# Spreading the first norm weights with whole-array products, and splitting the first two weight parts before the first copy

## The chip, the cores and the metric

One NeuronCore of one Trainium2 chip runs the whole program. The metric is the device time of one execution in microseconds (us); lower is better. Engines are named as in the profile: PE is TensorE (PEld its weight loads), DVE is VectorE, ACT is ScalarE, POOL is GpSimd, and SP is SyncE, which here only issues transfers.

## The reference, cut to what matters

Three transformer layers on one sequence of 256 tokens with 1024 features, all in fp32: attention and a squared-ReLU MLP, then two layers with modulation. The change touches the first lines of the first layer only:

```python
def rms_norm(x, gain):
    xf = x.astype(jnp.float32)
    y = xf * lax.rsqrt(jnp.mean(xf * xf, axis=-1, keepdims=True) + RMS_EPS)
    return (y * gain.astype(jnp.float32)).astype(x.dtype)

u = rms_norm(h, norm_mix_pre[layer])       # h = x, 256 x 1024
q, k, v = jnp.split(u @ w_qkv, 3, axis=-1) # w_qkv 1024 x 3072
```

## The kernel before

Every engine has its own written program, and semaphores order them. The tokens are two tiles (t = 0, 1) of 128 rows. Weights come in parts of 128 partitions by 1024 floats, 512 KB each, that SP loads in a fixed order into the slots of `w_raw`. ACT copies a part, rounded to fp32r, into `w_hi` (`split_part` of ACT, L721 to L727), and DVE subtracts that from the raw part and writes the rest to `w_lo` (`split_part` of DVE, L1160 to L1163). PE then multiplies high by high, high by rest and rest by high part. Activations are split in the same way: PE transposes the normed tile `xn` into PSUM (`norm_T`, L1917), ACT copies four blocks of it as the high part of `aT` (`norm_hi`, L776), and DVE takes the rest (`norm_lo`, L1170). A slot is loaded anew only when DVE has taken its rest.

The order of the work at the start, before the loops, is written out by hand on each engine:

- SP issues tile 0 of x, weight parts 0 and 1, tile 1 of x, parts 2 and 3, and then parts 4 and on as slots come free.
- POOL fills `eps` and `ones` (128x128 of 1.0), and then other constants, and counts `consts`.
- ACT issues the transfer of the 1024 norm weights (L811): half of them to partition 0 and half to partition 64 of `gain`. It loads its function table (L816), sums the squares of tile 0 (L737), takes ln (L822) and exp (L823) for `rstd`, splits part 0, copies the first four transposed blocks, splits part 1, and goes on to tile 1.
- PE runs three products of `ones` by `ones` (`warm_up(3)`, L2142). When the norm weights are there it spreads each half over all 128 partitions with a product that has one row: stationary `ones[q, :]`, moving `gain[q, 0, 0:CH]`, with q partition 0 for the first and partition 64 for the second (L2148). After one more product of ones it begins `first_entry`: transposes of tile 0, the products of parts 0 and 1 with it, transposes of tile 1, and the rest (L2022).
- DVE waits for the product of each half and for `rstd`, and writes `xn` = x * rstd * spread weights, read from PSUM (L1430), two instructions a tile. Between the tiles come the rests of part 0, of the first blocks of `aT`, and of part 1.

The lines around it on PE:

```python
warm_up(3)
pe.wait_ge(gain_loaded[0], 16)
for n in range(2):
    q = slice(n * P // 2, n * P // 2 + 1)
    pe.matmul(acc[:, 2 + n, :], ones[q, :], gain[q, 0, 0:CH], start=True, stop=True).then_inc(gain_spread, 1)
warm_up(1)
pe.wait_ge(consts, 2)
first_entry(U_QKV1, (acc[:, 0, :], acc[:, 1, :]))
```

Of the kernel before, what the change touches and what calls it, by code (L numbers as in the profile page):

```python
# [32 lines left out]
P = 128  # L33
# [4 lines left out]
CH = 512  # L38
# [72 lines left out]
def plus(base, i, per):  # L111

    return base if i is None else i * per + base


def block_program(nc, a, out):
    ctx = ExitStack()
    with ctx:
        def sb(name, shape, dt=F32):
            return ctx.enter_context(nc.sbuf_tensor(name, shape, dt))  # L120

        def ps(name, shape):
            return ctx.enter_context(nc.psum_tensor(name, shape, F32))

        def sem(name):
            return ctx.enter_context(nc.semaphore(name))
# [14 lines left out]
        gain = sb("gain", [P, 4, D])  # L141
# [3 lines left out]
        ones = sb("ones", [P, P])  # L145
# [66 lines left out]
        acc = ps("acc", [P, 4, CH])  # L212
# [55 lines left out]
        def rounded_part(v):  # L268

            return apart[v][0] if v in apart else w_hi[:, slot_of(v), :]  # L270
# [20 lines left out]
        def norm_banks(k, t):  # L291

            if k in NORMS_T:
                return [acc[:, 2 * t, :], acc[:, 2 * t + 1, :]]
            if k == 1:
                return [acc[:, 0, :], acc[:, 1, :]]
            if k == 2:
                return [tp[:, 0, :], tp[:, 1, :]]
            return [ub[:, 0, :], ub[:, 1, :]] if t else [tp[:, 0, :], tp[:, 1, :]]
# [2 lines left out]
        x_loaded = [sem("x_loaded0"), sem("x_loaded1")]  # L302
        rows_loaded = sem("rows_loaded")
        small_loaded = sem("small_loaded")
        gain_spread = sem("gain_spread")
        gain_loaded = [sem(f"gain_loaded{n}") for n in range(8)]
        w_loaded = [sem(f"w_loaded{n}") for n in range(SLOTS)]
# [101 lines left out]
        def blocks(w):  # L409
# [7 lines left out]
        gains = [a["norm_mix_pre"][0], a["norm_mix_post"][0], a["norm_ffn_pre"][0], a["norm_ffn_post"][0],  # L417
                 a["l0_mix_norm_2"], a["l0_ffn_norm_2"], a["l1_mix_norm_2"], a["l1_ffn_norm_2"]]
# [288 lines left out]
        def _(act):  # L707
            n_chain = [0]

            def chained(ins):  # L710
                n_chain[0] += 1
                ins.then_inc(act_chain, 1)
                act.wait_ge(act_chain, n_chain[0])
# [7 lines left out]
            def split_part(v, i=None, per=0):  # L721
                act.wait_ge(w_loaded[v % SLOTS], plus(16 * (v // SLOTS + 1), i, 16 * 2 * per // SLOTS))
                if v in before_in_slot:
                    act.wait_ge(w_used, before_in_slot[v] + 1)
                elif v >= SLOTS:
                    act.wait_ge(w_used, plus(v - SLOTS + 1, i, 2 * per))
                act.activation(rounded_part(v), w_raw[:, v % SLOTS, :], ACT.Copy).then_inc(hi_done, 1)  # L727
# [7 lines left out]
            def row_square(t, src):  # L735
                n_sq[0] += 1
                act.activation(squares[:, t, :], src, ACT.Square, accum_out=sums[:, t:t + 1]).then_inc(sq_done, 1)  # L737
# [34 lines left out]
            def norm_hi(k, t, groups=(0, 1)):  # L772

                for g in groups:
                    act.wait_ge(nT_done, 4 * k + 2 * t + g + 1)
                    act.activation(aT_hi[:, 4 * g:4 * g + 4, t * P:(t + 1) * P],  # L776
                                   norm_banks(k, t)[g].rearrange("p (b n) -> p b n", n=P), ACT.Copy).then_inc(n_hi, 1)
# [30 lines left out]
                act.wait_ge(w_used, parts_to(u + 2))  # L808
                act.activation(vtok[:, 0, n * CH:(n + 1) * CH], acc[:, 2 * n, :], ACT.Copy).then_inc(v_a, 1)

            act.dma_start(gain[0:P:P // 2, 0, 0:CH], gains[0].rearrange("(a n) -> a n", a=2)).then_inc(gain_loaded[0], 16)  # L811

            def first_norm(u):

                n_norm[0] += 1
                act.preload_act_table_set("natural_log_exp_and_others")  # L816
                act.wait_ge(consts, 1)
                for t in range(NT):
                    act.wait_ge(x_loaded[t], 16)
                    row_square(t, x[:, t, :])  # L820
                    act.wait_ge(sq_done, n_sq[0])
                    chained(act.activation(log_var[:, t:t + 1], sums[:, t:t + 1], ACT.Ln, scale=1.0 / D, bias=eps[:, 0:1]))  # L822
                    act.activation(rstd[:, t:t + 1], log_var[:, t:t + 1], ACT.Exp, scale=-0.5).then_inc(rstd_done, 1)  # L823
                    if t == 0:
                        split_part(2 * u)
                        norm_hi(0, 0, (0,))
                        split_part(2 * u + 1)
                norm_hi(0, 0, (1,))
                split_part(2 * u + 2)
                norm_hi(0, 1)  # L830
                split_part(2 * u + 3)

            first_norm(U_QKV1)
            act.activation(ones_r[:, :], ones[:, :], ACT.Copy)

# [310 lines left out]
        def _(dve):  # L1146
# [13 lines left out]
            def split_part(v, i=None, per=0):  # L1160
                dve.wait_ge(hi_done, hi_count(v, i, per))
                dve.tensor_tensor(rest_part(v), w_raw[:, v % SLOTS, :], rounded_part(v).bitcast(F32),  # L1162
                                  ALU.subtract).then_inc(lo_done, 1)  # L1163
# [26 lines left out]
            def norm_lo(t, q):  # L1190

                k = n_norm[0]
                n_norm[0] += t * q
                dve.wait_ge(n_hi, 4 * k + 2 * t + q + 1)
                part = (slice(None), slice(4 * q, 4 * q + 4), slice(t * P, (t + 1) * P))
                bank_lo(aT_lo[part], aT_hi[part], norm_banks(k, t)[q].rearrange("p (b n) -> p b n", n=P)).then_inc(n_lo, 1)
# [224 lines left out]
            def copy_v(u, n):  # L1421
                dve.wait_ge(w_used, parts_to(u + 2))
                dve.tensor_copy(vtok[:, 1, n * CH:(n + 1) * CH], acc[:, 2 * n + 1, :]).then_inc(v_v, 1)

            for t in range(NT):
                n_rstd[0] += 1
                dve.wait_ge(rstd_done, n_rstd[0])
                for c in range(2):
                    dve.wait_ge(gain_spread, c + 1)
                    dve.scalar_tensor_tensor(xn[:, t, c * CH:(c + 1) * CH], x[:, t, c * CH:(c + 1) * CH], rstd[:, t:t + 1],  # L1430
                                             acc[:, 2 + c, :], ALU.mult, ALU.mult).then_inc(xn_done, 1)
                if t == 0:
                    split_part(2 * U_QKV1)
                    norm_lo(0, 0)
                    split_part(2 * U_QKV1 + 1)
# [363 lines left out]
        def _(pe):  # L1799
# [339 lines left out]
            def warm_up(n):  # L2139

                for _ in range(n):
                    pe.matmul(ub[:, 0, :], ones[:, :], ones[:, :].unsqueeze(1).broadcast_to([P, 4, P]), start=True, stop=True)  # L2142

            warm_up(3)
            pe.wait_ge(gain_loaded[0], 16)
            for n in range(2):
                q = slice(n * P // 2, n * P // 2 + 1)
                pe.matmul(acc[:, 2 + n, :], ones[q, :], gain[q, 0, 0:CH], start=True, stop=True).then_inc(gain_spread, 1)  # L2148
            warm_up(1)
            pe.wait_ge(consts, 2)  # L2150
            first_entry(U_QKV1, (acc[:, 0, :], acc[:, 1, :]))

# [247 lines left out]
            for step, n in STICK_STEPS:  # L2400
# [27 lines left out]
                elif step == "W":  # L2428
# [3 lines left out]
                    for e in range(2):  # L2432
                        for b in range(3):
                            q = slice(e * SC + b * P, e * SC + (b + 1) * P)
# [37 lines left out]
```

## Time and profile before

| | us |
|---|---|
| median of 3 runs | 890.13 |
| lowest and highest | 889.53, 890.37 |
| the profiled execution's own time | 890.48 |
| its span in the profile | 888.4 |
| PE busy | 882.0 (99%) |
| DVE busy | 694.2 (78%) |
| ACT busy | 501.6 (56%) |
| POOL busy | 29.0 (3%) |

The span is that of one profiled execution; the rest of its own time, 2.1 us, lies around the span. Start times count from the start of the span. A row of the timeline merges neighbouring instructions of one kind: with x6 the length is that from the first's start to the last's end. A plain fp32 product appears as two records with the moving operand's 512 columns each.

### The profile page before, as it was taken

The numbers are of one execution on the slowest core, as the hardware profiler recorded it, in microseconds if no ns is written. First come the engines' busy times: TensorE is split into PE (matmuls) and PEld (weight loads), VectorE is DVE, ScalarE is ACT, GpSimd is POOL, SyncE is SP. The second block draws the span as 40 slices with busy tenths as digits, with TensorE's granted clock in tenths as the row PEclk, the third lists the DMA queues.
The fourth block names the chain that finished last, engine by engine and source line by source line (L and its number), as shares of the span: only waits on it lengthen the run. The fifth ranks groups of instructions, "written<-read, shape, count | busy, mean of one in ns | idle before, by whom it ended". The sixth has DMA issues, their size and how long they took to land.

```text
span 888.4 us, 13272 instructions
## 1 busy us (share of the span) xinstructions
PE 882.0 (99%) x4841; PEld 747.3 (84%) x4841; DVE 694.2 (78%) x735; ACT 501.6 (56%) x673; POOL 29.0 (3%) x52
## 2 busy tenths in 40 slices
PE   9999999999999999999999999999999999999998
PEld 5998878888888799979888888878777888888886
DVE  5698977988888987896888888687797875655655
ACT  6545665565555758756455455465775565545542
POOL 4000110000000100001000000010000000000000
PEclk9999999999999999999999999999999999999999
DMA  7979586899998385556988888636434366666661
GB/s 239 343 254 346 171 297 196 320 366 355 340 332 335 122 285 152 186 185 191 364 311 318 321 311 283 192 115 208 133 117 142 118 212 193 190 189 189 189 191 69
DMA packets 117093, 208.04 MB, mean 234 GB/s; under 512 B 7237, under 2 KB 81069, under 8 KB 111930
## 3 DMA queue, kind: packets, MB, share of 16 engines
q1 hardware_dynamic: 116566, 205.31, 67.9%
q10 hardware_dynamic: 292, 2.10, 0.7%
q8 instruction: 28, 0.46, 0.2%
q14 instruction: 15, 0.12, 0.0%
q0 software_dynamic: 192, 0.05, 0.0%
HBM read 206.39 MB, written 1.05 MB: 233 GB/s over the span
## 4 chain that ended last, share of the span: by engine, by line
PE 94%; DVE 3%; DMA 1%; issue 1%; ACT 0%; SPq 0%; DVEq 0%; POOL 0%; ACTq 0%; POOLq 0%
PE ub L1945 11%; PE tp L1945 10%; PE acc L1845 7%; PE acc L1846 7%; PE acc L1848 7%; PE ub L1947 5%; PE acc L1808 5%; PE tp L1947 5%; PE acc L1810 5%; PE acc L1809 5%; PE tp L1965 4%; PE acc L1931 3%; PE acc L1933 3%; PE acc L1932 3%; PE acc L1965 2%; PE acc L2022 1%
## 5 line engine op out<-in xcount | busy, mean ns | idle before, releaser
L1162 DVE TENSOR_TENSOR w_lo<-w_raw,w_hi 128x1024 fp32r<-128x1024 f32 x283 | 341.7, 1222 | 104.5 <-ACT w_hi L727 104.0
L727 ACT ACTIVATE w_hi<-w_raw 128x1024 fp32r<-128x1024 f32 x283 | 296.8, 1057 | 214.0 <-PE acc L1848 49.6
L1945 PE MATMUL tp<-aT,w_hi 128*128 128x512 f32 x432 | 135.9, 396 | 0.0
L1945 PE MATMUL ub<-aT,w_hi 128*128 128x512 f32 x432 | 135.4, 395 | 0.0
L1845 PE MATMUL acc<-w_hi,hT_hi 128*128 128x512 f32 x284 | 110.8, 390 | 0.7 <-DVE w_lo L1162 0.7
L1846 PE MATMUL acc<-w_lo,hT_hi 128*128 128x512 f32 x284 | 110.6, 389 | 0.0
L1848 PE MATMUL acc<-w_hi,hT_lo 128*128 128x512 f32 x272 | 105.8, 389 | 0.0
L1947 PEld LDWEIGHTS tp<-aT,w_lo 128*128 128x128 f32 x432 | 81.2, 188 | 19.2
L1947 PEld LDWEIGHTS ub<-aT,w_lo 128*128 128x128 f32 x432 | 81.1, 188 | 18.9
L1947 PE MATMUL tp<-aT,w_lo 128*128 128x256 f32 x432 | 84.9, 278 | 0.0
L1947 PE MATMUL ub<-aT,w_lo 128*128 128x256 f32 x432 | 84.9, 278 | 0.0
L1945 PEld LDWEIGHTS ub<-aT,w_hi 128*128 128x128 f32 x432 | 67.6, 189 | 2.0
L1945 PEld LDWEIGHTS tp<-aT,w_hi 128*128 128x128 f32 x432 | 65.8, 189 | 0.0
L1808 PE MATMUL acc<-w_hi,aT 128*128 128x512 f32 x160 | 64.4, 402 | 0.0
L1845 PEld LDWEIGHTS acc<-w_hi,hT_hi 128*128 128x128 f32 x284 | 53.3, 188 | 11.2 <-DVE w_lo L1162 0.7
L1810 PE MATMUL acc<-w_hi,aT 128*128 128x512 f32 x160 | 62.4, 390 | 0.0
L1809 PE MATMUL acc<-w_lo,aT 128*128 128x512 f32 x160 | 62.4, 390 | 0.0
L1846 PEld LDWEIGHTS acc<-w_lo,hT_hi 128*128 128x128 f32 x284 | 53.3, 188 | 10.1
L1848 PEld LDWEIGHTS acc<-w_hi,hT_lo 128*128 128x128 f32 x272 | 51.1, 188 | 10.8
L1372 DVE SCALAR_TENSOR_TENSOR mod<-ada_raw,silu_c,mod 128x2048 f32<-128x2048 f32 x24 | 56.3, 2346 | 0.2 <-DVE mod L1372 0.2
L1931 PE MATMUL acc<-aT,w_hi 128*128 128x256 f32 x192 | 55.3, 288 | 0.0
L1933 PE MATMUL acc<-aT,w_lo 128*128 128x256 f32 x192 | 54.3, 283 | 0.0
(330 smaller groups left out, 1309.8 us busy)
## 6 DMA issues: line engine op xcount, KB each, us to landing
ada_raw<-in_l_ada_w SPq DMA_DIRECT2D x24, 1024.0 KB, 6.5
w_raw<-in_l_ffn_w_gate SPq DMA_DIRECT2D x44, 512.0 KB, 4.6
w_raw<-in_l_ffn_w_up SPq DMA_DIRECT2D x44, 512.0 KB, 3.9
w_raw<-in_l_ffn_w_down SPq DMA_DIRECT2D x44, 512.0 KB, 3.6
w_raw<-in_w_up SPq DMA_DIRECT2D x32, 512.0 KB, 5.2
w_raw<-in_w_down SPq DMA_DIRECT2D x32, 512.0 KB, 5.6
scratch<-in_l_ada_w SPq DMA_DIRECT2D x14, 1024.0 KB, 7.8
w_raw<-in_attn_w_qkv SPq DMA_DIRECT2D x24, 512.0 KB, 6.8
```

The source lines that it names most:

```text
L727: act.activation(rounded_part(v), w_raw[:, v % SLOTS, :], ACT.Copy).then_inc(hi_done, 1)
L1162: dve.tensor_tensor(rest_part(v), w_raw[:, v % SLOTS, :], rounded_part(v).bitcast(F32), ALU.subtract).then_inc(lo_done, 1)
L1808: pe.matmul(outp, op_hi[:, k + n, q], wh[:, c], start=start and n == 0, stop=False)
L1809: pe.matmul(outp, op_hi[:, k + n, q], wl[:, c], start=False, stop=False)
L1810: last = pe.matmul(outp, op_lo[:, k + n, q], wh[:, c], start=False, stop=stop and n == 1)
L1845: pe.matmul(outp, operand[0][:, k, q], wh[:, c], start=start, stop=False)
L1846: last = pe.matmul(outp, operand[0][:, k, q], wl[:, c], start=False, stop=False)
L1848: last = pe.matmul(outp, operand[1][:, k, q], wh[:, c], start=False, stop=stop)
L1931: pe.matmul(outp, wh, aT_hi[:, b, :], start=b == 0, stop=False)
L1933: last = pe.matmul(outp, wl, aT_hi[:, b, :], start=False, stop=b == KB - 1)
L1945: pe.matmul(banks[f], rounded_part(v)[:, c[f]], aT[:, :, b, :], start=b == 0, stop=False)
L1947: last = pe.matmul(banks[f][:, 0:TOK], rest_part(v)[:, c[f]], aT_hi[:, b, :], start=False, stop=b == KB - 1)
```

## The change

Four edits, all at the start of the program:

1. DVE clears the whole of `gain[:, 0, :]` (128x1024 fp32) and counts a new semaphore, `gain_cleared`.
2. ACT waits for it, and then issues the transfer of all 1024 norm weights to partition 0, in place of two halves to two partitions.
3. PE runs two products of ones in place of three, spreads each half with a product that takes all 128 partitions (127 of them zeros), and runs no product of ones behind them.
4. ACT splits weight part 1 ahead of the first copy of transposed blocks, where it came behind it.

```diff
@@ -808,7 +809,8 @@
-            act.dma_start(gain[0:P:P // 2, 0, 0:CH], gains[0].rearrange("(a n) -> a n", a=2)).then_inc(gain_loaded[0], 16)
+            act.wait_ge(gain_cleared, 1)
+            act.dma_start(gain[0:1, 0, :], gains[0].rearrange("(a n) -> a n", a=1)).then_inc(gain_loaded[0], 16)
@@ -823,8 +825,8 @@
                     if t == 0:
                         split_part(2 * u)
+                        split_part(2 * u + 1)
                         norm_hi(0, 0, (0,))
-                        split_part(2 * u + 1)
@@ -1422,6 +1424,7 @@
+            dve.memset(gain[:, 0, :], 0.0).then_inc(gain_cleared, 1)
             for t in range(NT):
@@ -2141,12 +2144,11 @@
-            warm_up(3)
+            warm_up(2)
             pe.wait_ge(gain_loaded[0], 16)
             for n in range(2):
-                q = slice(n * P // 2, n * P // 2 + 1)
-                pe.matmul(acc[:, 2 + n, :], ones[q, :], gain[q, 0, 0:CH], start=True, stop=True).then_inc(gain_spread, 1)
-            warm_up(1)
+                pe.matmul(acc[:, 2 + n, :], ones[:, :], gain[:, 0, n * CH:(n + 1) * CH], start=True,
+                          stop=True).then_inc(gain_spread, 1)
             pe.wait_ge(consts, 2)
```

The order on ACT from its first transfer on, before (`nT_done` counts the groups of four transposed blocks, `w_loaded0` and `w_loaded1` the landings of weight parts 0 and 1):

```order
L811 DMA gain<-in_norm_mix_pre 2x512
L816 ACT_TABLE_LOAD
L737 ACTIVATE scratch,sums<-x 128x1024 [waits x_loaded0,consts]
L822 ACTIVATE log_var<-sums,eps 128x1 [waits sq_done]
L823 ACTIVATE rstd<-log_var 128x1 [waits act_chain]
L727 ACTIVATE w_hi<-w_raw 128x1024 [waits w_loaded0]
L776 ACTIVATE aT<-tp 128x4x128 [waits nT_done]
L727 ACTIVATE w_hi<-w_raw 128x1024 [waits w_loaded1]
L737 ACTIVATE scratch,sums<-x 128x1024 [waits x_loaded1]
```

and of the change:

```order
L813 DMA gain<-in_norm_mix_pre 1x1024 [waits gain_cleared]
L818 ACT_TABLE_LOAD
L738 ACTIVATE scratch,sums<-x 128x1024 [waits x_loaded0,consts]
L824 ACTIVATE log_var<-sums,eps 128x1 [waits sq_done]
L825 ACTIVATE rstd<-log_var 128x1 [waits act_chain]
L728 ACTIVATE w_hi<-w_raw 128x1024 [waits w_loaded0]
L728 ACTIVATE w_hi<-w_raw 128x1024 [waits w_loaded1]
L777 ACTIVATE aT<-tp 128x4x128 [waits nT_done]
L738 ACTIVATE scratch,sums<-x 128x1024 [waits x_loaded1]
```

The transfer has a wait ahead of it, and the second split stands ahead of the copy of the transposed blocks.

The order on PE from its first product on, before (`ub` and `acc` are banks of PSUM):

```order
L2142 MATMUL ub<-ones 128x512 [waits consts]
L2142 MATMUL ub<-ones 128x512 x2
L2148 MATMUL acc<-gain,ones 128x512 [waits gain_loaded0]
L2148 MATMUL acc<-gain,ones 128x512
L2142 MATMUL ub<-ones 128x512
L1917 MATMUL tp<-ident,xn 128x128 [waits xn_done,consts]
```

and of the change:

```order
L2145 MATMUL ub<-ones 128x512 [waits consts]
L2145 MATMUL ub<-ones 128x512
L2150 MATMUL acc<-gain,ones 128x512 [waits gain_loaded0]
L2150 MATMUL acc<-gain,ones 128x512
L1920 MATMUL tp<-ident,xn 128x128 [waits xn_done,consts]
```

One product of ones is gone ahead of the wait for the norm weights and one behind the two spreading products.

## Rows read from the trace of the kernel before

**Rows 1.** The page's first part: busy us, share of the span, instructions.
```profile
PE 882.0 (99%) x4841; PEld 747.3 (84%) x4841; DVE 694.2 (78%) x735; ACT 501.6 (56%) x673; POOL 29.0 (3%) x52
```

**Rows 2.** Waits of PE from 17 us to the end: us in total, times, longest.
```profile
PE acc L1845 <- DVE w_lo L1162: 0.7, 2, 0.5
PE acc L2166 <- issue: 0.3, 1, 0.3
```

**Rows 3.** The chain of waits, start to 130 us: start us, us, what.
```profile
1.02 5.31 PE ub L2142 x6
6.32 1.06 PE acc L2148 x4
7.38 1.06 PE ub L2142 x2
8.44 0.60 PE tp L1917 x4
...
10.61 0.14 issue
10.74 2.54 PE acc L2022 x10
13.28 1.07 PE ub L1917 x8
...
117.05 0.86 PE ub L2250 x2
```

**Rows 4.** Timeline of PE's weight loads and matmuls: start us, us, instruction.
```profile
3.74 0.34 PEld L2142 LDWEIGHTS ub<-ones 128*128 128x128 f32 x1 [0.52 <-issue]
4.59 0.34 PEld L2142 LDWEIGHTS ub<-ones 128*128 128x128 f32 x1 [0.52 <-issue]
...
5.44 0.88 PE L2142 MATMUL ub<-ones 128*128 128x512 f32 x1
```

**Rows 5.** Timeline of DVE, 0 to 15 us.
```profile
7.50 1.41 DVE L1430 SCALAR_TENSOR_TENSOR xn<-x,rstd,acc 128x512 f32<-128x512 f32 x2 [7.50 <-PE acc L2148]
8.82 1.22 DVE L1162 TENSOR_TENSOR w_lo<-w_raw,w_hi 128x1024 fp32r<-128x1024 f32 x1
10.63 1.23 DVE L1162 TENSOR_TENSOR w_lo<-w_raw,w_hi 128x1024 fp32r<-128x1024 f32 x1
12.24 1.41 DVE L1430 SCALAR_TENSOR_TENSOR xn<-x,rstd,acc 128x512 f32<-128x512 f32 x2 [0.38 <-ACT rstd L823]
```

**Rows 6.** Timeline of ACT, 0 to 12.5 us, and one row of 27 us.
```profile
0.74 1.11 ACTq L811 DMA_DIRECT2D gain<-in_norm_mix_pre  x1
1.88 1.28 ACT L816 ACT_TABLE_LOAD   x1 [1.88 <-issue]
5.90 0.20 ACT L823 ACTIVATE rstd<-log_var 128x1 f32<-128x1 f32 x1
6.00 1.04 ACT L727 ACTIVATE w_hi<-w_raw 128x1024 fp32r<-128x1024 f32 x1
9.06 0.60 ACT L776 ACTIVATE aT<-tp 128x512 fp32r<-128x512 f32 x1 [2.01 <-PE tp L1917]
9.55 1.05 ACT L727 ACTIVATE w_hi<-w_raw 128x1024 fp32r<-128x1024 f32 x1
10.50 1.05 ACT L737 ACTIVATE scratch<-x 128x1024 f32<-128x1024 f32 x1
12.00 0.20 ACT L823 ACTIVATE rstd<-log_var 128x1 f32<-128x1 f32 x1
...
27.10 1.06 ACT L727 ACTIVATE w_hi<-w_raw 128x1024 fp32r<-128x1024 f32 x1 [2.86 <-DMA w_raw<-in_attn_w_qkv]
```

**Rows 7.** DMA issues in 0 to 1.5, 2 to 2.5 and 6.5 to 7 us: us to landing.
```profile
x<-in_x SPq DMA_DIRECT2D x1, 512.0 KB, 3.6
...
x<-in_x SPq DMA_DIRECT2D x1, 512.0 KB, 6.5
...
mod<-in_l_ada_b POOLq DMA_DIRECT2D x1, 8.0 KB, 4.5
```

**Rows 8.** The queue of ACT's transfer, the last stretch with a packet of it (3.8 to 3.9 us).
```profile
q10 hardware_dynamic: 1, 0.00, 0.6%
```

**Rows 9.** Groups by shape: fills and copies near to the added one: xcount | busy us, mean ns.
```profile
L1408 DVE COPY scratch<-acc 128x512 f32<-128x512 f32 x2 | 1.4, 688 | 1.5 <-PE acc L2022 1.5
L666 POOL MEMSET rg_w<- 128x1024 f32 x1 | 1.0, 952 | 0.1
```

**Rows 10.** One stretch: us, busy of each engine, PEclk, DMA share, GB/s.
```profile
1.00:4.00 3.00, 2.98 (x4) 1.44 (x5) 0.00 (x0) 1.28 (x1) 2.36 (x8) 1.00 0.68 231
```

More of the change, by code:

```diff
@@ L304, in block_program @@
         small_loaded = sem("small_loaded")
+        gain_cleared = sem("gain_cleared")
         gain_spread = sem("gain_spread")
```

## The prediction

> **What bounds the kernel now.** I read the page's busy shares first: PE is busy 882.0 of 888.4 us, and no other engine comes near [rows 1]. Then the waits of PE alone: from 17 us to the end it waits 1.0 us in three places [rows 2]. So behind the start the time is PE's own work, and whatever time PE gains or loses at the start stays in the total. Then the chain of waits at the start [rows 3]: three products of ones from 1.02 to 6.32, the two spreading products to 7.38, one product of ones to 8.44, transposes, then a broken stretch until 13.28, where the transposes of tile 1 begin. From there the chain stays on PE. The place to predict is therefore the start of tile 1's transposes, 13.28 (modelled end of the work before; the engine's own start is at about 13.1).
>
> What sets that start? DVE. Its first instruction begins at 7.50, 0.12 us after the spreading products end; it then runs two `xn` instructions, three rests and again two `xn` with a single gap of 0.38 us, for tile 1's `rstd` [rows 5]. PE has idle moments before 13.1 and takes tile 1's `xn` when it comes. ACT had `rstd` of tile 0 ready at 6.10 [rows 6], 1.4 us before DVE could use it, because PE was still multiplying ones: that is the slack this change can reach. And tile 1's `rstd` is late because ACT sums its squares only from 10.50, behind a split that itself waited behind the copy of blocks at 9.06 [rows 6], though tile 1 of x had landed at about 2.18 + 6.5 = 8.7 [rows 7].
>
> **The clear and the transfer.** DVE does nothing before 7.50, so the clear itself costs DVE nothing; but the transfer waits for it, and ACT's table load waits behind the transfer. A DVE clear of 128x1024 does not occur in the trace. Near it stand a POOL clear of that size, 0.95 us, a DVE copy of half the size, 0.69 us, and a DVE subtraction of the full size, 1.22 us [rows 5, 9]; I bound it by 0.5 and 1.25 and take 1.05, nearest to the POOL clear. The Trainium skill, page "VectorE: DVE Perf Modes", section "Zero memsets can be issued as uint32 (trn2)", says that a memset takes one cycle per element whatever the type, which rules out that a clear runs at several elements a cycle; no run here shows it yet. If the engines begin at 0.74 as ACT does [rows 6], the clear ends at about 1.8 and the transfer is issued from 1.8 to 2.9, if it takes its 1.11 us again. The table load then runs from about 2.95 to 4.25, and tile 0 of x lands at 0.74 + 3.6 = 4.34 [rows 7]. So on ACT the 1.05 us are hidden, with only 0.1 us left; anything more (a clear of 1.25) pushes `rstd` from 6.10 by as much, and that is not yet the latest input of DVE (below). POOL's `ones` do not touch the same buffer; I cost their clash with the clear at nothing.
>
> When does the row land? Before, the last packet of ACT's queue came by 3.9 us [rows 8], 3.15 after the issue began; landing is not recorded, as nobody waited. From 1.8 on, the same delay gives 4.95, and with about 0.15 for the notice I take 5.1. Lower bound: tile 0 of x took 3.6 us for 128 times the data, so the small one may take under 3: 4.5. Upper: the 8 KB transfer that POOL issued at 6.8 under the same load took 4.5 us [rows 7]: 6.3.
>
> **PE.** The passes of a ones product start 0.855 us apart (3.74 to 4.59) [rows 4], while later fp32 products of the same size take 0.86 us for two, 0.43 each [rows 3]: a factor of two, so PE starts at the 1.2 GHz level although the granted clock of that stretch reads 1.00 [rows 10]. The last pass from 5.44 is only 0.88 long [rows 4] where 1.06 is usual, and from 6.32 records follow each other every 0.53. So I place the rise at about 6.15, after 5.1 us of unbroken products. With two products of ones, PE is done at 1.02 + 4 x 0.855 = 4.44. It then idles until 5.1, 0.66 us that it did not idle before. The spreading products before ran side by side: 1.06 us for both [rows 3]. Over the whole array they run one after the other: 1.06 each at the pace behind the rise (bounds 0.86, the later products, and 1.71, at the low level). The first: 5.1 to 6.15 at the low level is 61% of it, the rest 0.41, end 6.56; the second ends at 7.62. The removed product of ones behind them cost 1.06 on PE, but no one waited for it: the transposes waited for `xn` all the same.
>
> **DVE.** `xn` of the first half starts at 6.7, the second at 7.62 + 0.12 = 7.74 and ends at 8.48; before, the pair ended at 8.91. That is 0.43 earlier. The three rests take 8.91 to 11.86 before, 2.95 us, so now end at 11.43. The gap of 0.38 should go: ACT has part 0 split at 7.05 and part 1, by the reordering, at 8.1; the first blocks are transposed at about 8.25 and copied at 8.87, so the copy does not suffer from the split ahead of it, and x of tile 1 has landed, so its squares start at 8.87 in place of 10.50 and its `rstd` is ready at 10.6, well before 11.43. So `xn` of tile 1 starts at 11.43 in place of 12.24: 0.81 us earlier.
>
> **PE again.** Before tile 1's transposes PE has ten products of 0.225 us: they can start at about 9.1 with nothing to wait for between parts 0 and 1 (the 0.14 at 10.61 [rows 3] goes), then wait for the rest of part 1 until 11.43, and end at 11.9; tile 1's first half comes at 12.2. So PE is ready, and the transposes start 0.8 us earlier. What comes late next? ACT's copies and parts 2 and 3 move with the chain. Loads of part 4 and later wait for slots that DVE frees, so they move as well, and where ACT waits for a load, as for 2.86 us before 27.10 [rows 6], PE needs the part only some 5 us later, after the products of parts 6 and 7. I take nothing off there.
>
> The sum against the profiled execution is 890.48 - 0.8 = 889.7. That execution was 0.35 us above the median; against the median of 890.13 it is 889.35, which I forecast as 889.4. A measurement of this kernel can tell about 0.2% from no change, 1.8 us; so this gain would be within it.
>
> **A rule against it.** The rise of PE's clock is the weak point: of the 6.15 - 1.02 us in which PE worked without a pause before, it would now rest 0.66. The trace shows one rise, and not where it comes with a pause. The Trainium skill, page "TensorE: Matmul & The Clock Gate", section "What's actually happening", says that activity releases the throttle and that the measuring window runs free of the kernel's start. By that rule the rise comes at another point in each execution, and a pause can move it to a later one; the sentences that follow price this from rows.
>
> **The rivals.**
> *1. The clock rises late.* PE stays at the low level past the pause. The spreading products then take 3.42 us and end at 8.5, `xn` of the second half starts at 8.64, its end is 0.47 later than before and with the 0.38 gap gone tile 1's `xn` starts 0.1 later than before. If the clock rises there (9 to 10 us), that is all: +0.1 to +0.3. If it stays low beyond, the ten products take 4.3 us in place of 2.25, and PE reaches tile 1's transposes at about 14 in place of 13.1, transposes and products after that losing 0.5 us for each further us at the low level: +1.4 by 14 us, and over +1.8 only if it lasts to about 15. For it: the pause, and the shorter run of ones. Against: the pause is short, and full-array products run on both sides of it, 3.4 us of them ahead. Time: 890.3, or 891.5 in the longer form.
> *2. The row lands late.* At 6.3 in place of 5.1, with the clock up at 6.15, the products end at 8.4 and everything before is undone: 890.1. With the clock low, it is the longer form of rival 1. The row decides from 6.3 on.
> *3. The row lands early*, by 4.5. The products end at about 7.3, 0.3 earlier, and `xn` follows; or they run at 0.86 each, another 0.2 to 0.3. Time 888.9.
> *4. The lead is taken back* by a load or by PE's later waits, which are for rests of weights [rows 2]: 890.1. Against it are the spare us before each early part.
>
> **How the numbers follow.** The forecast (a lead of 0.5 to 0.9) has 0.45, rival 3 0.15, rival 1's short form 0.13 and its longer form 0.10, rival 2 0.07, rival 4 0.10. The range leaves out the far end of the longer form and a lead over 1.6: 888.5 to 891.0. Faster by over 1.8 us would need more than all of DVE's early wait for PE (1.4 us from 6.10) and the 0.38 gap together, 0.04; slower by that much needs the clock low to 15 us, 0.05; the rest, 0.91, is within.
>
> **What would show it.** DVE's clear of about 1.05 us from 0.74; ACT's transfer from 1.8; PE idle from 4.44 to about 5.1; spreading products ending near 6.6 and 7.6; `xn` of tile 1 at 11.4 with no gap ahead of it for `rstd`; two splits in a row on ACT from 6.0; tile 1's transposes at 12.3. Wrong would be: passes 0.855 apart behind 6.5 us, a pause of PE over 1.5 us, or a wait of `xn` of tile 1 for ACT.

## The result, and the profile after

The change made the kernel slower: 892.64 us (median of 18 runs, 890.0 to 894.45) against 890.29 us (18 runs, 889.53 to 891.07), a ratio of 1.0025 with a 95% interval of 1.0018 to 1.0031. I had forecast 889.4, with a range up to 891.0. Not only the middle moved: the runs of after spread over 4.45 us, three times as wide as those of before.

The profiled execution took 892.91 us, 2.43 more than that of before. The page shows the same work in a longer span: PE is busy 0.7 us more, and idle for 1.7 us more.

```profile
span 890.8 us, 13265 instructions
PE 882.7 (99%) x4837; PEld 748.3 (84%) x4837; DVE 694.8 (78%) x736; ACT 501.9 (56%) x673; POOL 29.0 (3%) x52
```

PE's waits from 17 us to the end add up to 1.2 us, as against the 1.0 of [rows 2]. So most of the loss arises before 17 us, and the chain of waits (start us, us, what) shows it; it answers to [rows 3].

```profile
1.02 0.92 DVE gain L1427
1.94 0.02 issue
1.97 4.71 DMA gain<-in_norm_mix_pre
6.68 0.04 issue
6.72 3.78 PE acc L2150 x4
10.51 1.96 PE tp L1920 x8
12.46 2.95 PE acc L2025 x12
15.41 0.87 PE ub L1920 x8
```

The clear, 0.92 us, then the transfer of 4 KB, 4.71 us, then the two spreading products, 3.78 us (1.06 for both before), then eight transposes in 1.96 (four took 0.60). Tile 1's transposes end the list: they start at 15.41, where they started at 13.28, 2.1 us later. The timeline of after (start us, us, instruction, and the idle time ahead of it) gives the engines beside it, as [rows 5, 6] did:

```profile
1.97 0.53 ACTq L813 DMA_DIRECT2D gain<-in_norm_mix_pre  x1
2.54 1.28 ACT L818 ACT_TABLE_LOAD   x1 [2.54 <-DVE gain L1427]
5.64 0.20 ACT L825 ACTIVATE rstd<-log_var 128x1 f32<-128x1 f32 x1
6.72 3.78 PE L2150 MATMUL acc<-gain,ones 128*128 128x512 f32 x4 [1.92 <-DMA gain<-in_norm_mix_pre]
8.14 1.06 ACT L728 ACTIVATE w_hi<-w_raw 128x1024 fp32r<-128x1024 f32 x1 [1.36 <-DMA w_raw<-in_attn_w_qkv]
10.54 0.75 DVE L1433 SCALAR_TENSOR_TENSOR xn<-x,rstd,acc 128x512 f32<-128x512 f32 x1 [0.87 <-PE acc L2150]
14.07 1.40 DVE L1433 SCALAR_TENSOR_TENSOR xn<-x,rstd,acc 128x512 f32<-128x512 f32 x2
15.25 1.04 PE L1920 MATMUL ub<-ident,xn 128*128 128x128 f32 x8
```

PE stands idle for 1.92 us until the row (the 1024 norm weights, all on partition 0) lands. `rstd` of tile 0 is ready at 5.84; the second half of tile 0's `xn` begins at 10.54. The gap ahead of tile 1's `xn` is indeed gone (no idle time at 14.07, 0.38 before), but the whole chain is 1.8 us late. The spreading products run at the 1.2 GHz level: their passes start 0.85 apart (7.74 and 8.59 in the next rows), as those of the ones did. The trace's own list of clock levels begins only when the clock rises: at 12.74 us here, at 6.02 in the trace of before.

```profile
7.74 0.34 PEld L2150 LDWEIGHTS acc<-gain,ones 128*128 128x128 f32 x1 [0.52 <-issue]
8.59 0.34 PEld L2150 LDWEIGHTS acc<-gain,ones 128*128 128x128 f32 x1 [0.52 <-issue]
```

### The profile page after: what moved, and what is told of

The parts are those of the page before. It is cut to its first block, busy times and chain, and to the rows that moved or that the text cites. A ratio compares the mean times of both kernels' runs of the same rounds, so it can differ in the third digit from the quotient of the medians.

```text
span 890.8 us, 13265 instructions
## 1 busy us (share of the span) xinstructions
PE 882.7 (99%) x4837; PEld 748.3 (84%) x4837; DVE 694.8 (78%) x736; ACT 501.9 (56%) x673; POOL 29.0 (3%) x52
## 3 DMA queue, kind: packets, MB, share of 16 engines
HBM read 206.39 MB, written 1.05 MB: 233 GB/s over the span
## 4 chain that ended last, share of the span: by engine, by line
PE 93%; DVE 4%; DMA 1%; issue 1%; ACT 1%; SPq 0%; DVEq 0%; ACTq 0%
PE ub L1948 11%; PE tp L1948 10%; PE acc L1848 7%; PE acc L1849 7%; PE acc L1851 7%; PE ub L1950 5%; PE acc L1811 5%; PE tp L1950 5%; PE acc L1812 5%; PE acc L1813 5%; PE tp L1968 3%; PE acc L1934 3%; PE acc L1936 3%; PE acc L1935 3%; PE acc L1968 2%; PE acc L2025 1%
```

## The experiments

Three theories were set against each other. **C**: the late row opens a pause of PE, the pause keeps the clock low, and the low clock is most of the loss. **R**: the late row costs it by itself. **S**: whole-array products in series cost it, at any clock. Each run below was timed beside the kernel before on the same chip; the medians of before in the three groups of several kernels were 890.26, 890.34 and 890.11. Each kernel ran eleven times. The ratios and intervals are those on record; they are not the ratio of the two medians, and differ from it by up to 0.0008.

**The third product of ones put back.** In the changed kernel:

```diff
-            warm_up(2)
+            warm_up(3)
             pe.wait_ge(gain_loaded[0], 16)
```

> The changed kernel with its third product of ones put back ahead of the wait for the norm weights. Theory C (the clock: PE's pause of about 2 us between the ones and the late row keeps it at the low level until about 10.5 us, and that is most of the loss): PE is busy to 6.32, the row lands at about 6.7, so the clock is up and the two spreading products take about 2.1 us and end near 8.8; xn of tile 1 begins near 12.5 and the time is 890.2 to 890.9. Theory R (the late row itself costs it, the clock little): about 892, as the changed kernel. Theory S (whole-array products one after the other are the cost, at any clock): 891.3 or more.

Measured: 890.82 us (890.0 to 891.3), ratio to before 1.0006 (0.9997 to 1.0015). The row landed as late as in after, at 6.71, but the clock was up:

```profile
6.76 1.98 PE L2150 MATMUL acc<-gain,ones 128*128 128x512 f32 x4 [0.86 <-DMA gain<-in_norm_mix_pre]
12.31 1.40 DVE L1433 SCALAR_TENSOR_TENSOR xn<-x,rstd,acc 128x512 f32<-128x512 f32 x2
13.12 1.30 PE L1920 MATMUL ub<-ident,xn 128*128 128x128 f32 x8
```

The same two products, after a wait that ended at the same time, take 1.98 us in place of 3.78, and tile 1's transposes start at 13.12, exactly as in the timeline of before (15.25 in that of after). One product of ones, work that no one uses, takes 1.8 us off the median of after (892.64 less 890.82; 1.7 by the two ratios to before). That is theory C, and it leaves about 0.5 us to R and S together, with whatever the new order of splits gives or takes.

**The wait alone.** In the kernel before (two halves, one-row products, three ones):

```diff
+            act.wait_ge(gain_cleared, 1)
             act.dma_start(gain[0:P:P // 2, 0, 0:CH], ...)
...
+            dve.memset(gain[:, 0, :], 0.0).then_inc(gain_cleared, 1)
```

> The kernel before with only the clear on DVE and the transfer's wait for it (two halves on two partitions, one-row products, three ones and one, the old order of splits). Theory C: the row lands near 6.7 in place of 4, but PE is covered by ones until 6.32, so the spreading products start 0.4 later: 890.5 to 890.8. Theory R: 892 or more. Theory S: 890.3, as before.

Measured: 891.6 us (891.17 to 892.28), ratio 1.0015 (1.0006 to 1.0024): between my figures for C and for R, 0.8 too slow for C as I had written it. The trace of this kernel shows a part of the reason, and it is the only trace here whose granted clock leaves 1.00 before PE's work is over. The view by stretches (stretch, us, busy and count of PE, PEld, DVE, ACT and POOL, granted clock, DMA share, GB/s):

```profile
9.00:12.60 3.60, 3.60 (x13) 2.71 (x13) 3.26 (x4) 2.41 (x4) 3.01 (x4) 0.53 0.71 249
12.60:16.00 3.40, 3.40 (x21) 2.77 (x20) 2.59 (x5) 2.93 (x8) 0.13 (x1) 1.00 0.80 259
```

The clock had risen, at 5.69 by the trace's list of levels, and it fell back to half from 9.10 to 12.52. What PE had done before it fell stands in the timeline: 0.78 us of pause, 1.1 us of one-row products, one product of ones.

```profile
6.95 1.13 PE L2151 MATMUL acc<-gain,ones 1*128 1x512 f32 x4 [0.78 <-DMA gain<-in_norm_mix_pre]
8.00 1.12 PE L2145 MATMUL ub<-ones 128*128 128x512 f32 x2
9.08 1.93 PE L1920 MATMUL tp<-ident,xn 128*128 128x128 f32 x8
```

So the clear and the wait cost 1.3 us over before even without the other edits. The fall is not in every run: the clock averaged over the whole run is 0.997 or 0.998 in four of the eleven (median 891.96) and 0.999 or 1.000 in the other seven (median 891.3). So about 1.0 us of the loss is there without a fall.

**That kernel with a fourth product of ones.**

```diff
-            warm_up(3)
+            warm_up(4)
```

> The kernel with only the clear and the wait (one-row products, two halves), with a fourth product of ones ahead of the row's wait. In the trace of that kernel the clock had risen by 6.0, PE paused from 6.2 to 6.9, the one-row products followed, and from 9.1 to about 12.6 PE ran at the low level again. If the pause with one-row products behind it took the clock down, covering it with ones keeps the clock up: tile 1's transposes begin near 13.8 in place of 14.5 and the time is 890.6 to 891.1, against 891.6. If the late row alone made that kernel slow, the time stays at 891.4 to 891.8.

Measured: 891.37 us (890.92 to 892.29), ratio 1.0017 (1.0008 to 1.0026). This does not tell the two figures apart. In its trace the clock stays up (eight transposes in 1.22 us where they took 1.93), but the four products of ones now last until 7.47 themselves, and the spread starts 0.45 us later than without the fourth, though the norm weights had landed at 6.65; tile 1's transposes begin at 14.29 against 14.54. In that execution the filler costs nearly what it saves. The average clock is 1.000 in all eleven runs, and still five of them lie at 891.86 or above. How much of the 1.3 us is clock stays open.

**The split order undone,** in the changed kernel: `norm_hi(0, 0, (0,))` between the two splits again.

> The changed kernel with the split of part 1 behind the first copy again. The order of splits was to take away the gap ahead of tile 1's xn, 0.38 us. Theories C, R and S all say: 0 to 0.8 us slower than the changed kernel, 892.6 to 893.4. If the split ahead of the copy is itself a cause of the loss, it is faster than the changed kernel by 0.3 or more.

Measured: 892.34 us (890.36 to 893.28), ratio 1.0021 (1.0012 to 1.0030): 0.3 below the median of after, well inside either spread. The order of the splits is not a cause of the loss that can be measured. Its profiled execution shows something else: the same transfer, issued at 1.96, landed after 3.56 us here and after 4.71 in after's. PE's pause was 0.77 us in place of 1.92, and the products were at the low level all the same; the clock rose at 9.45.

```profile
1.96 3.56 DMA gain<-in_norm_mix_pre
```

**The split order alone,** in the kernel before:

```diff
                         split_part(2 * u)
+                        split_part(2 * u + 1)
                         norm_hi(0, 0, (0,))
-                        split_part(2 * u + 1)
```

> The kernel before with only the order of ACT changed: the split of part 1 ahead of the first copy. The gap of 0.38 us ahead of tile 1's xn goes, if part 1 has landed by 7.05; nothing else moves: 889.8 to 890.1. If part 1 lands only at 8.1, as in the changed kernel's trace, the split ends at 9.2, the copy of the first blocks starts 0.1 later, and the rstd of tile 1 is still 0.7 earlier than before: the same 0.3 to 0.4 us.

Measured: 889.77 us (889.57 to 890.88) beside 890.34, ratio 1.0001 (0.9992 to 1.0010). It was run once more:

> The kernel before with only the split of part 1 ahead of the first copy, once more, beside the others of this batch. The first time it stood 0.57 us below the median of before: again 889.6 to 890.0 if that is real, 890.2 to 890.5 if it was not.

Measured: 890.21 us (889.24 to 891.08) beside 890.11, ratio again 1.0001 (0.9992 to 1.0010). The first lead was not repeated; the edit is worth nothing that can be told. The timeline of the first of the two shows where about half of the 0.38 us went:

```profile
8.19 1.06 ACT L727 ACTIVATE w_hi<-w_raw 128x1024 fp32r<-128x1024 f32 x1 [1.43 <-DMA w_raw<-in_attn_w_qkv]
9.79 1.20 PE L2022 MATMUL acc<-w_hi,aT 128*128 128x512 f32 x4 [0.70 <-ACT aT L776]
11.51 1.40 DVE L1430 SCALAR_TENSOR_TENSOR xn<-x,rstd,acc 128x512 f32<-128x512 f32 x2
```

Part 1 of the weights lands at 8.17, so the split waits 1.43 us for it, and the copy of the transposed blocks, ready since about 8.5, waits behind the split; PE then waits 0.70 us for the copy. The gap ahead of tile 1's `xn` is gone, and in its place stands a wait for a load: tile 1's `xn` begins 4.54 us behind tile 0's, where it was 4.74, so 0.2 us is left of it.

**The row ahead of the weights.** In the changed kernel SP issues the row between tile 0 of x and weight part 0:

```diff
             load_x(0)
+            sp.wait_ge(gain_cleared, 1)
+            sp.dma_start(gain[0:1, 0, :], ...).then_inc(gain_loaded[0], 16)
             proj_half(U_QKV1, qkv1, 0, 0)
...
-            act.wait_ge(gain_cleared, 1)
-            act.dma_start(gain[0:1, 0, :], ...).then_inc(gain_loaded[0], 16)
```

> The changed kernel with the row issued by SP right behind tile 0 of x and ahead of weight part 0, behind the same clear, which SP now waits for; weight parts 0 and on are issued about 0.8 us later. If the row is late because it stands behind the 1.5 MB of x and weights queued ahead of it, it lands by 4.6; then PE has no pause of more than 0.2 us, the clock rises near 6.15, the products end near 7.3 and the time is 889.5 to 890.3. If small transfers simply take about 4.7 us from their issue at this time, it lands at 6.7 and the time is 892 to 893.

Measured: 890.11 us (889.67 to 892.47), ratio 1.0002 (0.9993 to 1.0011); ten of eleven runs are at 891.05 or below. Same clear, same wait, same issue time (1.96), but nothing but tile 0 of x ahead in the transfers, and the row is there at 4.95:

```profile
1.96 0.31 SPq L505 DMA_DIRECT2D gain<-in_norm_mix_pre  x1
5.00 2.37 PE L2150 MATMUL acc<-gain,ones 128*128 128x512 f32 x4 [0.20 <-DMA gain<-in_norm_mix_pre]
```

It took 3.0 us from its issue, against 4.7. In this kernel SP held the weight parts back as well, so the run shows that the load ahead of a small transfer sets when it lands, and not how the engines share themselves out.

This kernel is nearly the case that I had forecast: the row at 4.95 (5.1 forecast), the clock up at 5.80 (6.15), tile 1's transposes at 12.40, 0.7 us earlier than before. The median is 0.15 below before, and not 0.8. The profiled execution, one of the two slowest, shows one way in which such a lead is lost: it took 891.05, 0.6 more than that of before. PE waits in it for a later norm:

```profile
PE acc L1920 <- DVE xn L1189: 1.0, 2, 0.7
378.77 5.80 DMA w_raw<-in_l_ffn_w_gate
```

The first line is of its waits from 17 us on, where before has no such wait; the second is of its chain of waits, and the `xn` of the longer of the two waits stands behind this load. Counted on DVE's instructions it is 0.8 ahead of before at 60 us, 0.6 ahead at 360 and 0.6 behind at 395. How often this happens, the other ten runs can't tell.

**Two products of ones and an early row.** In the kernel before, `warm_up(3)` becomes `warm_up(2)`, and nothing else:

> The kernel before with two products of ones ahead of the row in place of three, all else as before (one-row products side by side, one product of ones behind them). The row lands near 4.2, so there is no pause; the spreading products start at 4.5. If one-row products keep PE as busy to the clock as whole ones, the clock rises near 6.15, the spread is there at 6.2, xn starts at 6.3 and the time is 889.1 to 889.6. If they do not count, the clock rises later, and the time is 890.5 to 892 with a wide spread between executions.

Measured: 890.98 us (889.33 to 892.21), ratio 1.0007 (0.9998 to 1.0016). The runs fall in two groups: two at 889.33 and 889.78, the other nine from 890.92 up. There is no pause in its trace, the norm weights having landed at 4.01, before the ones end, and yet the clock is late:

```profile
4.73 2.08 PE L2148 MATMUL acc<-gain,ones 1*128 1x512 f32 x4
6.73 2.08 PE L2142 MATMUL ub<-ones 128*128 128x512 f32 x2
8.60 1.92 PE L1917 MATMUL tp<-ident,xn 128*128 128x128 f32 x8
10.35 2.23 PE L2022 MATMUL acc<-w_hi,aT 128*128 128x512 f32 x4
```

The clock rises at 12.59, and everything until then runs at half pace. PE was as busy as in before; what replaced whole-array ones from 4.8 to 6.8 was one-row products. They fill time but did not raise the clock here. The last kernel below has whole-array products in that place, and none of its 22 runs is above 890.4; it differs in other things too.

**One-row products between ones,** an attempt at beating both: two ones ahead, two behind, and the new split order.

> The kernel before with the one-row products side by side put between two products of ones ahead and two behind them, and the split of part 1 ahead of the first copy: an attempt at beating both. The row is there at 4.4; at the low level the two products take 1.7 us and end near 6.2, when rstd is ready too; xn starts at 6.3 in place of 7.5. PE is busy with ones to about 8.0. With the clock up near 6.2: 888.9 to 889.4. If the two ones behind delay the first transposes (xn's first half is there at 7.05): 889.4 to 889.9. If one-row products do not count for the clock: 890.5 or more.

Measured: 891.39 us (888.87 to 892.4), ratio 1.0005 (0.9996 to 1.0015). Again two groups: four runs from 888.87 to 889.75 and seven from 891.35 up. Its lowest run is the lowest of all on record. The profiled execution is one of the seven: the clock rises at 10.54, the ones behind the spread run from 6.81 to 10.52 at half pace, and the transposes wait behind them. That the four fast runs are those in which the clock rose early is likely, but no trace shows one of them.

**The row on one partition, no clear.** In the kernel before the whole row goes to partition 0, and both one-row products read it there:

> The kernel before with the whole row on partition 0 and both one-row products there, so they can't run side by side; no clear, no wait, three ones and one. The second product ends 1.06 us later than before if the pace behind the rise is kept, xn of the second half starts at 8.5 in place of 8.2: 0.2 to 0.4 us slower than before, 890.5 to 890.7 (theory S would have 891.3 or more from this alone).

Measured: 890.72 us (890.05 to 891.35), ratio 1.0008 (0.9999 to 1.0017). The products took 1.98 us one after the other where they had taken 1.06 side by side. It is 0.4 slower at the median, as expected, and not above what can be told: by the interval it is 1.5 us at most. So theory S is worth little, and the last kernel, which has whole-array products in series and is the fastest, says the same. This trace also shows how fast the row can be: 4 KB to one partition, issued at 0.74 with only tile 0 of x beside it, landed at 2.60.

**The idea without the wait.** In the changed kernel the transfer itself writes the norm weights to 32 partitions, at the start, and DVE clears the other 96; the stationary operand holds 1/32 (`spread` is 128 columns of scratch that POOL fills). PE waits for the clears and for POOL, and the transfer waits for nothing:

```diff
-            act.wait_ge(gain_cleared, 1)
-            act.dma_start(gain[0:1, 0, :], ...)
+            act.dma_start(gain[0:32, 0, :], gains[0].partition_broadcast(32)).then_inc(gain_loaded[0], 16)
...
-            dve.memset(gain[:, 0, :], 0.0).then_inc(gain_cleared, 1)
+            dve.memset(gain[32:64, 0, :], 0.0).then_inc(gain_cleared, 1)
+            dve.memset(gain[64:P, 0, :], 0.0).then_inc(gain_cleared, 1)
...
             warm_up(2)
+            pe.wait_ge(gain_cleared, 3)
             pe.wait_ge(gain_loaded[0], 16)
...
-                pe.matmul(acc[:, 2 + n, :], ones[:, :], gain[:, 0, n * CH:(n + 1) * CH], start=True,
+                pe.matmul(acc[:, 2 + n, :], spread[:, :], gain[:, 0, n * CH:(n + 1) * CH], start=True,
```

> The changed kernel without its wait: the row is broadcast by the transfer to partitions 0 to 31 (128 KB), issued by ACT at the start as before; DVE clears only partitions 32 to 127, in two instructions, and the stationary operand is 1/32 in place of 1 in the spreading products, which still take all 128 partitions. If the wait is what made the changed kernel slow, the rows land near 4.5 to 5, there is no pause over 0.5 us, the clock rises near 6, the products end near 7.3: 889.4 to 890.2. If whole-array products after only two products of ones are slow in themselves, 891 or more.

Measured: 889.34 us, eleven runs from 889.29 to 889.58, ratio 0.9992 (0.9983 to 1.0001). And again:

> The kernel that loads the norm weights to 32 partitions without a wait, once more, to see if its lead is real: 889.2 to 889.6 and all executions within 0.5 us of each other if xn of tile 0 waits for rstd and no longer for PE, so that the point at which the clock rises does not matter; 889.8 to 890.5 with a spread as wide as that of before if the first result was luck.

Measured: 889.56 us (889.18 to 890.37) beside 890.68, ratio 0.9990 (0.9981 to 0.9999). The spread is narrower than that of before, though the second time it was 1.2 us and not the 0.5 I had named. The timeline of the first:

```profile
0.75 0.41 ACTq L814 DMA_DIRECT2D gain<-in_norm_mix_pre  x1
4.59 2.00 PE L2153 MATMUL acc<-gain,scratch 128*128 128x512 f32 x4
5.09 1.06 ACT L740 ACTIVATE scratch<-x 128x1024 f32<-128x1024 f32 x1 [2.61 <-DMA x<-in_x]
6.83 1.41 DVE L1435 SCALAR_TENSOR_TENSOR xn<-x,rstd,acc 128x512 f32<-128x512 f32 x2 [3.73 <-ACT rstd L826]
11.03 1.40 DVE L1435 SCALAR_TENSOR_TENSOR xn<-x,rstd,acc 128x512 f32<-128x512 f32 x2
12.17 1.03 PE L1922 MATMUL ub<-ident,xn 128*128 128x128 f32 x8
```

The norm weights for 32 partitions, 128 KB, landed at 4.37. They are not free: tile 0 of x lands 0.7 us later than in before, at 5.0, and `rstd` with it. But the spread is ready at 6.6, before `rstd` at 6.79, so `xn` no longer waits for PE. That is, as I read it, why the point at which the clock rises matters less, and why the runs agree. By its median this is the fastest of the kernels that were run, 0.8 and 1.1 us ahead of before, about 0.1%: beyond noise in one of the two comparisons and at its edge in the other.

**The profiled executions side by side** (us; landings by the semaphore events, rises by the list of clock levels, starts by the timelines; one execution each, and the rise differs from one to the next):

| kernel | norm weights landed | spread begins | clock rises | tile 1's transposes | time |
|---|---|---|---|---|---|
| before | 4.17 | 6.25 | 6.02 | 13.12 | 890.48 |
| third product of ones back | 6.71 | 6.76 | 5.14 | 13.12 | 890.82 |
| wait alone | 6.90 | 6.95 | 5.69, falls 9.10, rises 12.52 | 14.54 | 892.15 |
| row ahead of the weights | 4.95 | 5.00 | 5.80 | 12.40 | 891.05 |
| 32 partitions, no wait | 4.37 | 4.59 | 4.78 | 12.17 | 889.29 |
| split order undone | 5.52 | 5.57 | 9.45 | 14.00 | 891.56 |
| after | 6.68 | 6.72 | 12.74 | 15.25 | 892.91 |
| two ones, one-row products | 4.01 | 4.73 | 12.59 | 14.34 | 891.43 |

## Why the prediction was wrong

The forecast was 0.8 us faster; after is 2.35 us slower at the median. Two steps failed: the landing of the row, and with it the rise of the clock. Two of the three signs that I had named for being wrong came: passes 0.85 apart behind 6.5 us, and a pause of PE over 1.5 us. Step by step:

- **What bounds it**: right in the main. The time is decided before tile 1's transposes. They came 2.1 us late, and the profiled executions differ by 2.4. But I had written that whatever PE gains or loses at the start stays in the total, and that holds only to some tenths: counted on DVE's instructions, after is 2.0 behind at 60 us and 2.4 from 395 us on, and the kernel with the row ahead of the weights lost its lead on the way.
- **The clear**: 1.05 us expected, 0.91 measured. DVE began at 1.02 and not at 0.74, so it ended at 1.93 in place of 1.8. The Trainium skill, page "VectorE: DVE Perf Modes", section "Zero memsets can be issued as uint32 (trn2)", has a clear take one cycle per element whatever the type. The traces agree in so far as no clear was faster than 0.91 us for 1024 elements a partition, over 32, 64 or 128 partitions alike; only fp32 was cleared, so what it says of the type no run here shows.
- **ACT behind it**: better than expected. With one partition to write, the issue took 0.53 us in place of 1.11, and `rstd` was ready at 5.84.
- **The landing of the row**: the first step that failed. I took 5.1 and an upper bound of 6.3; it landed at 6.68. I carried the delay of before, 3.15 us from issue to last packet [rows 6, 8] and 0.15 for the notice, over to an issue 1.2 us later. For before itself that was about right: the semaphore events of its trace have the landing, which I took for not recorded, at 4.17, 3.43 us behind the issue. But before, the transfer was issued beside tile 0 of x; at 1.97, SP had begun to issue two weight parts ahead of it too. From issue to landing it took 4.71, 3.56, 4.75, 4.94 and 4.69 us in five kernels with the clear, 3.0 us when the weights were held behind it, and 1.86 us for the same row issued at 0.74.
- **The clock**: the second step that failed, and the larger one in time. I placed the rise at 6.15 and had the first spreading product 61% done by then. The pause was 2.3 us by the count that gave me 0.66 (from 4.44, where the next pass would have begun; 1.92 in the profile's row), and the clock rose only at 12.74. The spread took 3.78 us (2.5 expected), the transposes nearly double, and the first of the products behind them too. Putting one product of ones back took 1.8 of the 2.35 us away. The step failed because the first one did: with the row at 4.95 the clock rose at 5.80, and ten of eleven runs were at 891.05 or below.
- **Series in place of side by side**: 1.06 us more on PE was expected; one-row products in series took 0.9 more and cost 0.4 at the median, within noise.
- **The gap ahead of tile 1's xn**: it went, as forecast, but the step that called it a gain was wrong. I had the split of part 1 run from 7.05, and so the part landed by then, without a row that says so; it landed at 8.12, the split ahead of the copy waited for it, and alone the edit brought nothing that can be told. In before it had landed at 7.38.
- **The rivals**: what happened is rival 2 ending in the longer form of rival 1, a case that I named and gave a part of 0.07, with 0.10 for the longer form. Its price, 1.4 us, was too small because I had worked it out with the row at 5.1, where the spread ends at 8.5; it ended at 10.5. My range, up to 891.0, left out even that price of 891.5. The two rivals were not independent as I had counted them: a later row is a longer pause, and the longer pauses here went with the later rises.

The spread of after probably has the same source, though only one of its executions was traced. Before, ones covered PE without a break, so only the point of the rise varied; in after both it and the landing do. The Trainium skill, page "TensorE: Matmul & The Clock Gate", section "What's actually happening", has the window running free of the kernel's start, and the traces agree: three products of ones from 1.02 on, identical work, took 5.31, 5.15, 4.88, 4.78, 4.53 and 4.29 us in six profiled executions, with the rise at 6.02, 5.69, 5.14, 4.96, 4.45 and 3.97.

## What to carry to other kernels

Work that only keeps PE busy has a price when it is taken away: before removing a filler, find the latest time at which the transfer behind it can land, and ask what the clock does until then. Here one product of ones, 1.7 us of work for nothing, was worth 1.8 us. A small transfer that is moved behind a wait must be priced with the bytes that will be queued ahead of it at its new issue time, not with its old delay. And where a wait guards a clear, see if the transfer can be written so that it need not wait: clear only what the transfer does not touch. Here that was the fastest kernel.

## What the runs showed that I had not expected

- One-row products did not stand in for whole-array ones at the start: with them in place of a product of ones, without any pause, PE stayed at the low level until 12.59 us, and nine of eleven runs were 0.58 us or more above the median of before.
- The clock can fall again after it has risen: granted 0.53 on average over 9.0 to 12.6 us, after a pause of 0.78 us and 1.1 us of one-row products.
- The views show a granted clock of 1.00 from the first microsecond, though passes 0.85 us apart show the low level. The trace's list of clock levels has no entry ahead of the rise, and the view takes the empty stretch for 1.00. The first entry is the rise: each microsecond by which it came earlier took half a microsecond off the three products of ones.
- 128 KB issued at 0.75 landed at 4.37 us, sooner than 4 KB issued at 1.97, which landed at 6.68. The same 4 KB issued at 0.74 landed at 2.60.
